# Tensors laid at one remainder modulo 512 bytes, VectorE's segments ahead of the steps on y, and the scan's heads in turn

## What is computed

```python
for i in range(DEPTH):                      # 2
    h = rms_norm(x, mix_pre_g[i])
    m = ssd_mixer(h, ...) if i % 2 == 0 else shortconv_mixer(h, ...)
    x = x + rms_norm(m, mix_post_g[i])
    x = x + rms_norm(conv_ffn(rms_norm(x, ffn_pre_g[i]), ...), ffn_post_g[i])

# ssd_mixer: 32 heads of 64 in 8 groups, state 128
z, xbc, dt = split(h @ w_in); xbc = silu(causal_dwconv(xbc, conv_w, conv_b))
seg = a_cs[..., :, None] - a_cs[..., None, :]
lmat = exp(where(tri, seg, -inf)); cb = C @ B^T                 # per group
y_diag = (cb * lmat) @ (x * dt)
states = B^T @ (exp(a_cs[-1] - a_cs) * x * dt);  prev = scan of states over the chunks
y = y_diag + (C @ prev) * exp(a_cs) + D * x
return rms_norm(y * silu(z), norm_w) @ w_out
```

## Time and profile before

| | us |
|---|---|
| median of 3 runs | 1379.48 (1379.45 to 1379.69) |
| the profiled execution | 1379.67 |
| its span | 1377.9 |
| TensorE busy | 1356.2 (98%) |
| VectorE busy | 787.6 (57%) |
| ScalarE busy | 569.1 (41%) |
| GpSimd busy | 24.4 (2%) |

### The profile page before, as it was taken

One profiled execution on the slowest core, in us unless ns is written; L12 is line 12 of the kernel. 1 busy time (PEld: TensorE's weight loads), 2 busy tenths in 40 slices (PEclk: granted clock), 3 DMA queues, 4 the chain that ended last, 5 costly groups with the idle time before them and its releaser, 6 DMA issues.

```text
span 1377.9 us, 15929 instructions
## 1 busy us (share of the span) xinstructions
PE 1356.2 (98%) x6474; PEld 1120.6 (81%) x6474; DVE 787.6 (57%) x1139; ACT 569.1 (41%) x875; POOL 24.4 (2%) x28
## 2 busy tenths in 40 slices
PE   8999999999999999999999999999999999999998
PEld 7877787777888988888888888888898888888886
DVE  4878887787623666655642256445466656554223
ACT  6666545566324534333331163222453433333112
POOL 0000000000000000000000000000000000000000
PEclk9999999999999999999999999999999999999999
DMA  5432233332242233333333313333223333333331
GB/s 150 154 107 78 91 107 107 111 109 72 77 137 62 62 107 108 92 96 103 92 125 98 113 48 93 102 96 113 86 62 108 108 92 92 101 98 122 95 104 61
DMA packets 181773, 135.70 MB, mean 98 GB/s; under 512 B 5645, under 2 KB 169893, under 8 KB 180677
## 3 DMA queue, kind: packets, MB, share of 16 engines
q1 hardware_dynamic: 181653, 134.62, 32.4%
q10 hardware_dynamic: 48, 0.07, 0.0%
HBM read 132.51 MB, written 2.16 MB: 98 GB/s over the span
## 4 chain that ended last, share of the span: by engine, by line
PE 91%; ACT 7%; issue 1%; DMA 0%; DVE 0%; SPq 0%; DVEq 0%
PE bank L831 19%; PE bank L833 19%; PE bank L832 19%; PE bank L894 9%; PE bank L893 9%; PE bank L892 9%; PE bank L1012 1%; ACT w_hi L345 1%; ACT mask L407 1%; PE bank L1020 1%; ACT feat L397 1%; PE bank L1002 1%; PE bank L869 1%; ACT L403 1%; ACT L407 1%
## 5 line engine op out<-in xcount | busy, mean ns | idle before, releaser
L831 PE MATMUL bank<-h_hi,w_hi 128*128 128x512 f32 (+1 forms) x1352 | 515.6, 381 | 0.0
L833 PE MATMUL bank<-h_lo,w_hi 128*128 128x512 f32 (+1 forms) x1352 | 513.1, 380 | 0.0
L832 PE MATMUL bank<-h_hi,w_lo 128*128 128x512 f32 (+1 forms) x1352 | 513.0, 379 | 0.0
L568 DVE TENSOR_TENSOR w_lo<-w_raw,w_hi 128x1024 fp32r<-128x1024 f32 x228 | 278.3, 1223 | 335.4 <-ACT w_hi L345 335.4
L345 ACT ACTIVATE w_hi<-w_raw 128x1024 fp32r<-128x1024 f32 x228 | 238.4, 1053 | 203.6 <-PE bank L894 180.6
L833 PEld LDWEIGHTS bank<-h_lo,w_hi 128*128 128x128 f32 x1352 | 254.2, 188 | 49.6
L832 PEld LDWEIGHTS bank<-h_hi,w_lo 128*128 128x128 f32 x1352 | 254.3, 188 | 48.7
L831 PEld LDWEIGHTS bank<-h_hi,w_hi 128*128 128x128 f32 x1352 | 254.5, 188 | 48.5
L892 PE MATMUL bank<-w_hi,hid_hi 128*128 128x512 f32 x416 | 165.0, 397 | 0.0
L894 PE MATMUL bank<-w_hi,hid_lo 128*128 128x512 f32 x416 | 164.8, 396 | 0.0
L893 PE MATMUL bank<-w_lo,hid_hi 128*128 128x512 f32 x416 | 164.8, 396 | 0.0
(11 more groups left out here) (147 smaller groups left out, 964.6 us busy)
## 6 DMA issues: line engine op xcount, KB each, us to landing
w_raw<-in_ffn_w_up SPq DMA_DIRECT2D x88, 512.0 KB, 3.8
w_raw<-in_ssd_w_in SPq DMA_DIRECT2D x48, 512.0 KB, 4.0
w_raw<-in_ffn_w_down SPq DMA_DIRECT2D x44, 512.0 KB, 3.5
w_raw<-in_sc_w_in SPq DMA_DIRECT2D x24, 512.0 KB, 3.7
acs_b<-acs_dram SPq DMA_DIRECT2D x8, 1024.0 KB, 6.3
w_raw<-in_ssd_w_out SPq DMA_DIRECT2D x16, 512.0 KB, 3.5
w_raw<-in_sc_w_out SPq DMA_DIRECT2D x8, 512.0 KB, 3.6
x_tok<-in_x SPq DMA_DIRECT2D x4, 512.0 KB, 4.9
```

What stands on the lines that cost most here:

```text
L568: nc.vector.tensor_tensor(w_lo[slot(u)][:], w_raw[:, u % 2, :], w_hi[slot(u)][:].bitcast(F32), ALU.subtract).then_inc(w_lo_done, 1)
L831: nc.tensor.matmul(dst, wh, xh, start=start, stop=False)
L832: nc.tensor.matmul(dst, wl, xh, start=False, stop=False)
L833: return nc.tensor.matmul(dst, wh, xl, start=False, stop=stop)
```

## The change

It has three parts.

First, homes. Small tensors that took 32 to 128 bytes each are put into one tensor of 128 columns (`small`, and `few` inside the SSD stage), and `pad` and `cpad` are widened to whole multiples of 128 columns (only the columns used before are read and written). All large tensors then begin at the same remainder modulo 512:

| remainder modulo 512 | before | after |
|---|---|---|
| x_tok, h_hi, h_lo, w_raw, w_hi and w_lo of slots 0 to 2, ident | 128 | 128 |
| tri, par | 160 | 128 |
| w_hi and w_lo of slots 3 and 4, g_row, r_row, scaled, cpad | 192 | 128 |
| acc, gated, side, hid_hi, hid_lo | 224 | 128 |
| acs_b, mask, feat, pad | 192 | 128 |
| cbm, b_tok, xdt, xdd, prev, e_row, z_act, square, total | 224 | 128 |
| acs_tok, dt_tok | 352 | 128 |
| y_hi, y_lo, xn_tok, pages, wdt_hi, wdt_lo | 416 | 128 |

Second, the order on VectorE and ScalarE: from group 1 on, `segments` stands in the group before, ahead of the steps on y; the exp of the mask and the two small ones stand there too, ahead of `y_hi`, and the four pieces of `e_row` behind the squares, as `exps_row`. Group 0 keeps its order. Third, the scan: the loops over chunks and the two heads of a tile are exchanged.

```diff
-        ident, ones, tri = sb("ident", [P, P]), sb("ones", [P, 1]), sb("tri", [P, P])
+        ident, tri = sb("ident", [P, P]), sb("tri", [P, P])
         par = sb("par", [P, 4, P])
...
+        small = sb("small", [P, P])
...
+        ones, eps, unread, q_tok = col(1), col(1), col(1 + DEPTH), col(C)
+        sums, rest_sum, root, r_post = col(4, 2 * C), col(4, C), col(4, C), col(4, C)
+        x_sums, r_pre_tok = col(3, C), col(3, C)
...
-            pad = sb("pad", [P, 2, SSD_CW - 1 + T], stack=ssd)
+            pad = sb("pad", [P, 2, T + P], stack=ssd)
...
-            cpad = sb("cpad", [P, CW - 1 + T], stack=rest)
+            cpad = sb("cpad", [P, T + P], stack=rest)
...
             def exps(g):
                 act.wait_ge(seg_done, g + 1)
                 nc.scalar.activation(mask[:], mask[:], ACT.Exp).then_inc(exps_done, 1)
+                nc.scalar.activation(decay[:], decay[:], ACT.Exp).then_inc(exps_done, 1)
...
+            def exps_row(g):
+                if g:
+                    act.wait_ge(y_step, 8 * (g - 1) + 7)
                 for j in range(XG):
...
                 if g:
-                    exps(g)
                     conv_in(g, 2, g * XG)
...
                 splits_to(GU * g + 5 + 4)
+                if g < GROUPS - 1:
+                    exps(g + 1)
                 for j in range(XG):
...
+                if g < GROUPS - 1:
+                    exps_row(g + 1)
...
             for g in range(GROUPS):
-                if g:
-                    segments(g)
-                    splits_to(GU * g + 4)
...
                 splits_to(GU * g + 5 + 4)
+                if g < GROUPS - 1:
+                    segments(g + 1)
...
+                if g < GROUPS - 1:
+                    splits_to(GU * (g + 1) + 4)
...
-                    for h in range(HX):
-                        for c in range(C):
+                    for c in range(C):
+                        for h in range(HX):
```

More of the change, by code:

```diff
@@ L165, in build, with col @@
         w_lo = [sb(f"w_lo{n}", [P, D], F32R) for n in range(3)]
-        ident, ones, tri = sb("ident", [P, P]), sb("ones", [P, 1]), sb("tri", [P, P])
+        ident, tri = sb("ident", [P, P]), sb("tri", [P, P])
         par = sb("par", [P, 4, P])
[L168 to L171, removed]
+        small = sb("small", [P, P])
+        small_at = [0]
+        def col(n, per=1):
+            at = small_at[0]
+            small_at[0] = at + n * per
+            assert small_at[0] <= P
+            return small[:, at:at + n * per].rearrange("p (n c) -> p n c", n=n) if per > 1 else small[:, at:at + n]
+        ones, eps, unread, q_tok = col(1), col(1), col(1 + DEPTH), col(C)
+        sums, rest_sum, root, r_post = col(4, 2 * C), col(4, C), col(4, C), col(4, C)
+        x_sums, r_pre_tok = col(3, C), col(3, C)
         with ExitStack() as ssd:
@@ L186, in build @@
             square, total = sb("square", [P, 2, T], stack=ssd), sb("total", [P, T], stack=ssd)
-            decay, c_decay = sb("decay", [P, HG, C - 1], stack=ssd), sb("c_decay", [P, HG, C - 1], stack=ssd)
+            few = sb("few", [P, P], stack=ssd)
+            decay, c_decay = (few[:, n * HG * C:n * HG * C + HG * (C - 1)].rearrange("p (h c) -> p h c", h=HG) for n in range(2))
+            d_col = few[:, 2 * HG * C:2 * HG * C + IT]
             acs_tok, dt_tok = sb("acs_tok", [P, C, HEADS], stack=ssd), sb("dt_tok", [P, C, HEADS], stack=ssd)
-            d_col = sb("d_col", [P, IT], stack=ssd)
             with ExitStack() as late:
@@ L395, in conv_in @@
                 u = bank[GROUP_BANKS[f]][:]
-                nc.scalar.copy(pad[:, f % 2, SSD_CW - 1:], u)
+                nc.scalar.copy(pad[:, f % 2, SSD_CW - 1:SSD_CW - 1 + T], u)
                 nc.scalar.activation(feat[:, f, :], u, ACT.Identity, bias=one(col_ssd_b(page_tile)),
@@ L407, in exps @@
                 nc.scalar.activation(mask[:], mask[:], ACT.Exp).then_inc(exps_done, 1)
+                nc.scalar.activation(decay[:], decay[:], ACT.Exp).then_inc(exps_done, 1)
+                nc.scalar.activation(c_decay[:], acs_b[:].rearrange("p h (c l) -> p h c l", l=P)[:, :, 0:C - 1, P - 1],
+                                     ACT.Exp).then_inc(exps_done, 1)
+            def exps_row(g):
+                if g:
+                    act.wait_ge(y_step, 8 * (g - 1) + 7)
                 for j in range(XG):
@@ L428, in _ @@
                     exps(g)
+                    exps_row(g)
                 conv_in(g, 3, g * XG + 1)
@@ L524, in ffn_up @@
                 act.wait_ge(gate_in, n + 1)
-                nc.scalar.activation(acc[:], cpad[:, CW - 1:], ACT.Identity, bias=one(col_ffn_b(layer, t)),
+                nc.scalar.activation(acc[:], cpad[:, CW - 1:CW - 1 + T], ACT.Identity, bias=one(col_ffn_b(layer, t)),
                                      scale=one(col_ffn_w(layer, CW - 1, t))).then_inc(acc_done, 1)
@@ L537, in sc_in @@
                 act.wait_ge(gate_in, n + 1)
-                nc.scalar.activation(acc[:], cpad[:, CW - 1:], ACT.Copy, scale=one(col_sc_w(CW - 1, i))).then_inc(acc_done, 1)
+                nc.scalar.activation(acc[:], cpad[:, CW - 1:CW - 1 + T], ACT.Copy, scale=one(col_sc_w(CW - 1, i))).then_inc(acc_done, 1)
                 splits_to(u + 6)
@@ L774, in ffn_up @@
                 dve.wait_ge(unit_done, u + 1)
-                nc.vector.tensor_tensor(cpad[:, CW - 1:], bank[banks[0]][:], r_row[:, 0, :], ALU.mult).then_inc(gate_in, 1)
+                nc.vector.tensor_tensor(cpad[:, CW - 1:CW - 1 + T], bank[banks[0]][:], r_row[:, 0, :], ALU.mult).then_inc(gate_in, 1)
                 splits_to(u + 4)
@@ L795, in sc_in @@
                 dve.wait_ge(unit_done, u + 2)
-                nc.vector.tensor_tensor(cpad[:, CW - 1:], side[:], bank[banks[1]][:], ALU.mult).then_inc(gate_in, 1)
+                nc.vector.tensor_tensor(cpad[:, CW - 1:CW - 1 + T], side[:], bank[banks[1]][:], ALU.mult).then_inc(gate_in, 1)
                 splits_to(u + 5)
```

3 lines of the change are left out of this document (removed).

## The result

The changed kernel takes 1355.05 us (median of 5 runs, 1354.71 to 1355.58) against 1379.65 us, a ratio of 0.982 with a 95% interval of 0.981 to 0.983. The forecast was 1353.8 us, 1345 to 1367. The profiled execution has a span of 1353.8 us, 24.1 less than the 1377.9 of before, and the page's first table begins with

The account below looks back on a forecast made before the run. TensorE bounds the kernel, busy 1356.2 of 1377.9 us, so only matmul pace and its few waits count. Homes 18.6, order 6.7 and scan 0.4 sum to 25.7 us off: 1379.5 - 25.7 = 1353.8 us, range 1345 to 1367.

Parts of the forecast that it names:

- Units: FFN and short-conv input stages: 2472 matmuls of 512 columns, slots 3 and 4 reach the pace of slots 0 to 2, 7.4 us off.
- Projections: Output projections: 1632 matmuls go from 233.7 to 226.7 ns, price carried over from the input stages, 11.6 us off.
- Half units: Matmuls of 256 columns behind a boundary, weights in slots 3 and 4: slower at equal remainders, 0.6 us on.
- dt projection: At the start, 24 matmuls with weights at 416 modulo 512: 0.2 us off.
- The row predicted for group 4: SSD stage, links over VectorE and ScalarE from group 3 to C·B (L984): starts at 213.02 instead of 213.97, 0.95 us off.
- what is late next: SSD stage, in front of C·B: the same row still holds TensorE, which waits some 1.2 us.
- A load takes a microsecond more: Bound for the SSD order: with this and L614 keeping 1.26 us, 0.95 off per group becomes -1.1, 8 us on.
- projections don't gain: Rival for the output projections: their operands, hid or y stationary, gain nothing from equal remainders; 1365.4 us, chance 0.12.
- the homes do nothing: Rival for all matmuls: pace bound to something else of slots 3 and 4; 1372.4 us, chance 0.05.
- equal remainders are the bad case in the projections: Rival for the output projections: equal remainders slow them, 1376.3 us with one step up (0.02), 1387 with two (slower: 0.03).
- The regrouping that costs: Rival in the SSD stage: the new row comes out 1 to 2 us longer; 1360.5 to 1368 us, chance 0.13.
- The wait that vanishes: Rival in the SSD stage: no wait at C·B (L984), the scan counts in each group; 1345.8 us, chance 0.09.

## Why the prediction was right, step by step

**The homes: 18.6 us forecast, 17.4 measured alone.** Units: 7.4 forecast, 7.0 found. Every slot has 226.7 ns, and slot 0, which had 228 before, has lost its settling. Projections: 11.6 forecast by carrying the price over from the units, 11.0 found. The step without a row of its own held: 226.7 ns there too, with stationary and streamed operand exchanged. It came out 0.6 short since the last projection, from which the 7.1 ns were taken, is the one that gained most: 3.74 us over 528 matmuls are 7.1 ns, 2.34 over the 384 of the first only 6.1. Half units: +0.6 forecast and found. The 0.2 us for the dt projection weren't there: from its first matmul to its last, with what stands between, it is 6.87 us before and 6.88 after. C·B of group 0 starts at 45.15 us instead of 45.17, with a wait at the start that was 1.3 instead of 0.6 us.

**The order: 6.7 us forecast for seven groups, 6.2 measured,** alone and in the changed kernel (295.01 us from C·B of group 0 to that of group 7, now 288.84). The row predicted for group 4, from the start of `w_lo`, against the one above:

| link | forecast | measured |
|---|---|---|
| w_lo, segments | 1.13 + 3.22 | 1.13 + 3.22 |
| steps on y, with GpSimd in the last | 5.95 | 5.94 |
| y_hi and square, e_row | 1.19 + 2.18 | 1.18 + 2.17 |
| conv_in of tile 0 | 1.14 | 1.28 |
| w_hi, w_lo of unit 3 | 1.06 + 1.26 | 1.08 + 1.23 |
| load of unit 5 | 4.01 | 4.00 |
| w_hi of unit 5 to C·B | 3.57 | 3.58 |
| sum | 24.71 | 24.81 |

The mis-sized link of this row is `conv_in`, 0.14 us longer than the 1.14 of the earlier trace rows; why is not known, no run was made for it. `segments` lost the 1.1 us of meeting GpSimd, and the load of unit 5 is waited for, 0.41 us, as was said. The prediction called this row what is late next, and taking its link of unit 3 away removed the whole wait; that the taps, held by the same link, would be nearly as late it didn't say. "A load takes a microsecond more" did not happen.

**The scan: 0.45 us in the last group forecast, 0.46 found,** from C·B of group 7 to the projection (18.40, now 17.94), and nothing in the others. The 32 instructions take 1.97 us instead of 2.57 with the heads in turn, and VectorE's state step sets L1039. Alone, on the old order, it is worth 0.41 in every group.

**The rivals.** That projections don't gain, that the homes do nothing and that equal remainders are the bad case in the projections fall by the run of the homes alone. What the prediction drew from the two quoted places of the Trainium skill, that the homes would be worth nothing, falls too: the same 512 columns at the same clock follow each other after 226.7 or after 233 ns. The rule that TensorE never waits on another engine is not tested by it. The regrouping that costs falls by the run of the order alone. The wait that vanishes was wrong for this kernel, and it can be had: with unit 3's split moved up the time is 1345.4 against the rival's 1345.8. That the two agree so closely is luck. The sum of the homes under it is 1.2 us too good, and a group got 2.32 us shorter (42.06 to 39.74) and not 1.64 + 0.45: the 1.64 is the idle time of the earlier trace rows, counted from the modelled end of a matmul, while from start to start TensorE lost 1.79 us (2.02 less the pace of 0.23). What the prediction put too narrowly is the rule itself: it spoke of the remainder modulo 512, and 256 is what counts, which for these homes is the same.

## What to carry to other kernels

Before tuning a matmul stream that is already dense, compare the starts of many equal matmuls: two paces that return with the buffers point to where the buffers lie, and equal remainders modulo 256 bytes for both operands were worth 1.3% here, at no instruction more. When a wait is shortened by moving work, write down the new row of links up to the same instruction; its sum told the gain to 0.1 us a group, and its weakest link (a split that stood behind work it didn't need) told the next change. Gains on two sides of a join don't add: measured alone, the parts promised 27.0 us and gave 24.5.

## What was not expected of the hardware

- Matmuls of 512 columns in this format follow each other after 226.7 ns when both operands start at the same remainder modulo 256 bytes, and after 232 to 234 ns at distances of 32, 64, 96, 128 and 192. Why is open.
- With 256 columns it is the other way: 120 ns at equal remainders or 256 apart, 118 to 120 at 128 apart, about 118 at 32 and 64 apart, and 113 in two stretches at 64. None of the runs tells why.
- One of three matmuls with an operand out of line slows its neighbours too: 236 ns behind its own, 228 to 230 behind the other two, where 226.7 is the pace without it.
- VectorE's step of 512 columns on two SBUF tensors takes 0.69 us alone and 1.66 beside GpSimd's addition, one of 12 columns 0.17 and 1.26: the price, 0.97 and 1.09 us, is close to what is left of GpSimd's instruction (1.10 in the first case), not a share by size.
